# Seven block products for the up projection of MLP groups 2 to 4, and weight sums made by accumulating transfers

## Chip, core and metric

One core of a Trainium2 chip runs the whole kernel. The metric is device time in microseconds (us) from launch to end of one execution; a profiled execution is recorded beside the timed ones. TensorE is PE in the profile (PEld its weight loads), VectorE is DVE, ScalarE is ACT, GpSimd is POOL, SyncE is SP.

## What is computed

One decoder layer on 512 tokens of width 1024, all float32. The part after the token mixing is what changes most:

```python
merged = (sigmoid(ga + b_ga) * (y_a @ w_branch[0])
          + sigmoid(gb + b_gb) * (y_b @ w_branch[1])
          + sigmoid(gc + b_gc) * (y_c @ w_branch[2]))
x = layer_norm(ALPHA * x + merged @ w_o, ln1_g, ln1_b)
h = square(relu(x @ w_up))                       # w_up (1024, 4096)
x = layer_norm(ALPHA * x + h @ w_down, ln2_g, ln2_b)   # w_down (4096, 1024)
```

`ga`, `gb` and `gc` are gate columns of an input projection of x; y_a, y_b, y_c come from a convolution, a gated recurrence and an attention into 256 memory tokens.

## The kernel before

**Operands.** Each float32 operand is split into a high part (rounded, made by ACT) and a low part (the rest, made by DVE), and each product is three matmuls, high by high, high by low, low by high (`three`, L1781 to L1783). So every matmul of a projection shows under these three lines, whatever the stage. Weights come in slabs of 1 MiB (128 partitions x 2048 floats): SP loads a slab into `raw`, ACT makes `w_hi` (L960 in the MLP), DVE makes `w_lo` (L1081), and PE waits for the count `slab_lo` before it uses the slab (`slab`, L1776).

**Seven products.** Where a product of two-by-two blocks is computed with seven block products m1 to m7 instead of eight, sums of weight blocks and sums of activation blocks ("forms") are needed. Gates 2 and 3 (`seven_gate`, `seven_product`, L2044) are computed so, with sums of weight blocks made by DVE (L1358, L1366 and others) in `gate_a` and `gate_c`. There a product is 48 matmuls of 256 columns. All down projections of the MLP are computed so too: 7 products of 2 rows of 12 matmuls, 512 columns wide.

**MLP.** It runs over 4 groups of 1024 of the 4096 hidden columns. In each group PE does the up projection as eight plain tiles (`up_tile`, L2160: 24 matmuls of 512 columns each, all 512 tokens), then the seven down products (`down`, L2193). Of the first group's up projection the first four tiles are computed in token halves, beside the layer norm. ACT squares each pair of tiles (L1003 to L1015), DVE makes the forms of a quarter of the group from them (`forms`, L1608 to L1611) and their low parts, and DVE also makes four sums of 1 MiB weight blocks for the down products (`sum_of`, L1602: x12 on `small`, x4 with `raw`). A down product's result leaves PSUM by `down_add` (L1642), in the order m1, m5, m6, m3, m2, m7, m4. In the last group the order of rows is `LAST_ROWS`, and DVE takes the layer norm's statistics (L1648) as each block is complete. Weight slots are four in the MLP, three in the gates.

**POOL.** It makes the split of the memory keys and values for each of two halves (L619, L621), clears `merged` (L639), scales the residual by ALPHA once layer norm 1 has been transposed (L643, counted in `resid_ready`, for which every `down_add` waits), and at the end scales and shifts five of the eight output half blocks (L650, L653). It issues no transfer. All transfers are SP's, in program order, each behind the wait for its buffer.

Of the kernel before, what the change touches and what calls it, by code (L numbers as in the profile page):

```python
# [24 lines left out]
P = 128  # L25
T = 512
# [28 lines left out]
S_MLP, N_MLP = S_OUT + 4, 11  # L55
# [21 lines left out]
UP_SLABS = 4  # L77
# [5 lines left out]

SHARED = ((2, 0), (2, 1), (3, 0), (3, 1), (0, 0))
# [3 lines left out]
LAST_ROWS = (("m3", 0), ("m2", 0), ("m3", 1), ("m2", 1), ("m7", 0), ("m4", 0), ("m7", 1), ("m4", 1))  # L88


def made(g, name, r):

    at = 2 * PRODUCTS.index(name) + r
    if g == G_MLP - 1 and (name, r) in LAST_ROWS:
        at = 2 * len(PRODUCTS) - len(LAST_ROWS) + LAST_ROWS.index((name, r))
    return 2 * len(PRODUCTS) * g + at + 1


SUMS = ("m5", "m6", "m7", "m4")


def aside(g, name):

    return g == G_MLP - 1 and name == "m2"
# [39 lines left out]
def down_bank(g, name):  # L144
    return 2 if g == G_MLP - 1 and name == "m4" else DOWN_BANK[name]


def down_slab(g, name):
    return S_MLP + g * N_MLP + UP_SLABS + PRODUCTS.index(name)

# [34 lines left out]
def build(nc, x, mem, lower_bounds, w_in, conv_w, hg_norm_w, w_mem_k, w_mem_v, w_branch, b_gate, w_o,  # L185
          ln1_g, ln1_b, w_up, w_down, ln2_g, ln2_b, out):
    ds = bass.ds
    with ExitStack() as ctx:
# [49 lines left out]
        h_forms = two[:, 4:6, :].rearrange("p a (b t) -> p (a b) t", t=T // 2)[:, 0:7, :]  # L238
# [19 lines left out]
        form_of = dict(m7=gate_a[:, 0:1024], m6=gate_a[:, 1024:2048], m5=gate_b[:, 0:1024], m3=gate_b[:, 1024:2048])  # L258
        small = sb("small", [P, 9 * 1024])
# [18 lines left out]
        raw_a = small[:, 0:SLAB]  # L278
        raw_b = small[:, SLAB:2 * SLAB]
        raw_c = small[:, 2 * SLAB:3 * SLAB]  # L280
        late = small[:, 8192:9216].rearrange("p (c t) -> p c t", t=256)
        early = two[:, 4, :].rearrange("p (c t) -> p c t", t=256)
        h_kept = small[:, 8192:9216].rearrange("p (j t) -> p j t", j=PAIRS)
        aside_hi, aside_lo = (t[:, 0:PAIRS, :].rearrange("p k c -> p (k c)") for t in (x_hi, x_lo))
# [51 lines left out]
        a_landed, b_landed = sem("a_landed"), sem("b_landed")  # L336
        c_landed, sums_made = sem("c_landed"), sem("sums_made")
        up_done, up_read = sem("up_done"), sem("up_read")
        h_squared, form_step, forms_made = sem("h_squared"), sem("form_step"), sem("forms_made")
        forms_hi, forms_ready = sem("forms_hi"), sem("forms_ready")  # L340
        kept_hi, kept_ready = sem("kept_hi"), sem("kept_ready")
        down_done, down_read = sem("down_done"), sem("down_read")
# [15 lines left out]
        def moved_par(n, e):  # L358
            return [bank[DOWN_BANK[name] + r] for name, r, m, f in MOVED if (m, f) == (n, e)][0]
# [10 lines left out]
        def mlp_round(g):  # L370
            return g * 4 + 20

# [23 lines left out]
        wdn = w_down[0].rearrange("(k two p) c -> p two k c", two=2, p=P)  # L396

        def down_block(g, k, n):

            return wdn[:, k - 1, g * PAIRS:(g + 1) * PAIRS, (n - 1) * WID:n * WID]  # L400
# [14 lines left out]

        def direct_slab(g, d):

            return S_MLP + g * N_MLP + d if d < UP_SLABS else down_slab(g, "m2")

        @block.sync  # L420
        def _(sp):
# [116 lines left out]
            sp.wait_ge(gate_done, seven_done(2, "m6", 1))  # L538
            par_load(2, ln2_g)
            par_load(3, ln2_b)  # L540
            def direct(g, d, src, k):

                n = R_MLP + 5 * g + d
                if n < R_MLP + 2:
                    sp.wait_ge(slab_lo, S_MLP - 2 + d + 1)
                else:
                    before = 5 * g + d - 2
                    sp.wait_ge(slab_lo, direct_slab(before // 5, before % 5) + 1)
                sp.dma_start(raw[:, n % 2, :].rearrange("p (k c) -> p k c", k=k), src).then_inc(slab_landed[n % 2], 16)

            def up_load(g, j):
                direct(g, j, wup[:, :, g * D + j * 256:g * D + (j + 1) * 256], KD)

            for g in range(G_MLP):
                up_load(g, 0)
                up_load(g, 1)
                if g == 0:
                    sp.wait_ge(merged_split, KD)
                else:
                    sp.wait_ge(slab_lo, down_slab(g - 1, "m4") + 1)  # L560
                sp.dma_start(as_block(raw_a), down_block(g, 1, 1)).then_inc(a_landed, 16)
                if g:
                    sp.wait_ge(sums_made, 4 * g)
                sp.dma_start(as_block(raw_b), down_block(g, 2, 2)).then_inc(b_landed, 16)
                if g == 0:
                    sp.wait_ge(x1_ready, 2 * TB)
                else:
                    sp.wait_ge(slab_lo, down_slab(g - 1, "m7") + 1)
                sp.dma_start(as_block(raw_c), down_block(g, 1, 2)).then_inc(c_landed, 16)
                up_load(g, 2)  # L570
                up_load(g, 3)
                direct(g, 4, down_block(g, 2, 1), PAIRS)
# [17 lines left out]
        def _(pool):  # L590
# [25 lines left out]

            for half in range(2):
# [1628 lines left out]
```

## Time and profile before

| | us |
|---|---|
| median of 3 runs | 820.9 |
| lowest, highest | 820.64, 821.03 |
| the profiled execution, its own time | 820.31 |
| its span, first to last instruction | 818.5 |

The span is what the trace covers; about 1.8 us of the profiled execution's time lie around it. PE is busy 99% of the span at a granted clock of 0.997 of full speed, DVE 67%, ACT 46%, POOL 4%. Matmul durations in the trace overlap, since matmuls are pipelined and their ends are modelled: 390 ns is given for one of 512 columns, while the next starts much sooner. What a matmul costs is the distance between starts. The chain of work that ended last, followed back from the end, lies on PE almost throughout; that of waits lists, for each pair of instructions, how long an engine stood idle before one until the other had finished.

### The profile page before, as it was taken

The page shows a single profiled execution, that of the slowest core. Times are in us where ns is not written, and L with a number is a line of the kernel's source. Part 1 is how long each engine was busy: PE and PEld are TensorE (multiplying, and loading weights), DVE is VectorE, ACT ScalarE, POOL GpSimd, SP SyncE. Part 2 cuts the span into 40 slices and gives each one's busy share as a digit, 9 for nine tenths or more (in the row PEclk, how much of TensorE's full clock was granted, in tenths as well). Part 3 has the DMA queues.
Part 4 walks back from the last instruction along what each step waited for, and adds up shares of the span by engine and source line. Part 5 has one row for each costly group of instructions (what it writes and reads, how often), then busy time and mean ns, then how long its engine had stood idle before and what let it go on. Part 6 is the DMA issues. An engine that isn't in the chain of part 4 may idle for free.

```text
span 818.5 us, 10651 instructions
## 1 busy us (share of the span) xinstructions
PE 809.0 (99%) x4347; PEld 698.9 (85%) x4347; DVE 551.1 (67%) x612; ACT 375.3 (46%) x439; POOL 32.1 (4%) x40
## 2 busy tenths in 40 slices
PE   8999999999999999999999999999999999999996
PEld 8889888899888889989988899888888888888885
DVE  4647655477358628768567686986588658855887
ACT  5558324493435324443453036643554355435533
POOL 1100100000001000000000010000000000000006
PEclk9999999999999999999999999999999999999998
DMA  9641313313120730620647116028102810280002
GB/s 309 207 154 52 103 52 102 102 51 102 51 76 28 257 103 1 223 87 1 207 154 246 63 39 219 1 68 293 51 1 70 289 52 1 73 287 1 1 0 104
DMA packets 64207, 87.64 MB, mean 107 GB/s; under 512 B 1661, under 2 KB 43686, under 8 KB 64166
## 3 DMA queue, kind: packets, MB, share of 16 engines
q1 hardware_dynamic: 64166, 87.06, 31.6%
q8 instruction: 30, 0.49, 0.2%
q14 instruction: 11, 0.09, 0.0%
HBM read 84.96 MB, written 2.10 MB: 106 GB/s over the span
## 4 chain that ended last, share of the span: by engine, by line
PE 98%; DVE 1%; DMA 1%; SPq 0%; DVEq 0%; issue 0%
PE bank L1781 31%; PE bank L1782 31%; PE bank L1783 31%; DMA two<-in_mem_dram 1%; PE bank L1997 0%; PE bank L1947 0%; PE bank L1918 0%; PE bank L2117 0%; PE bank L1808 0%; PE bank L2000 0%; PE bank L1985 0%; PE bank L1949 0%; PE bank L1954 0%; PE bank L1975 0%; PE bank L1800 0%; DVE smx L1648 0%
## 5 line engine op out<-in xcount | busy, mean ns | idle before, releaser
L1781 PE MATMUL bank<-x_hi,w_hi 128*128 128x512 f32 (+1 forms) x672 | 245.7, 366 | 0.0
L1782 PE MATMUL bank<-x_lo,w_hi 128*128 128x512 f32 (+1 forms) x672 | 244.6, 364 | 0.0
L1783 PE MATMUL bank<-x_hi,w_lo 128*128 128x512 f32 (+1 forms) x672 | 244.5, 364 | 0.0
L1783 PEld LDWEIGHTS bank<-x_hi,w_lo 128*128 128x128 f32 x672 | 126.8, 189 | 20.0
L1781 PEld LDWEIGHTS bank<-x_hi,w_hi 128*128 128x128 f32 x672 | 126.8, 189 | 19.9
L1782 PEld LDWEIGHTS bank<-x_lo,w_hi 128*128 128x128 f32 x672 | 126.9, 189 | 19.5
L1781 PE MATMUL bank<-w_hi,y_hi 128*128 128x512 f32 x296 | 115.5, 390 | 0.0
L1783 PE MATMUL bank<-w_hi,y_lo 128*128 128x512 f32 x296 | 115.2, 389 | 0.0
L1782 PE MATMUL bank<-w_lo,y_hi 128*128 128x512 f32 x296 | 115.2, 389 | 0.0
L1081 DVE TENSOR_TENSOR w_lo<-raw,w_hi 128x2048 fp32r<-128x2048 f32 (+2 forms) x35 | 71.5, 2046 | 35.1 <-ACT w_hi L960 25.3
L1783 PEld LDWEIGHTS bank<-w_hi,y_lo 128*128 128x128 f32 x296 | 55.6, 188 | 11.5
L1781 PEld LDWEIGHTS bank<-w_hi,y_hi 128*128 128x128 f32 x296 | 55.6, 188 | 11.5
L1782 PEld LDWEIGHTS bank<-w_lo,y_hi 128*128 128x128 f32 x296 | 55.6, 188 | 11.4
L1081 DVE TENSOR_TENSOR w_lo<-small,w_hi 128x2048 fp32r<-128x2048 f32 (+1 forms) x28 | 59.8, 2138 | 3.4 <-ACT w_hi L686 1.4
L960 ACT ACTIVATE w_hi<-raw 128x2048 fp32r<-128x2048 f32 x17 | 32.6, 1918 | 63.0 <-PE bank L1783 41.8
L1076 DVE TENSOR_TENSOR w_lo<-raw,w_hi 128x2048 fp32r<-128x2048 f32 x22 | 50.4, 2296 | 15.6 <-ACT w_hi L665 15.3
L960 ACT ACTIVATE w_hi<-small 128x2048 fp32r<-128x2048 f32 x24 | 45.8, 1906 | 10.2 <-PE bank L1783 10.2
L1642 DVE TENSOR_TENSOR two<-two,bank 128x512 f32<-128x512 f32 x56 | 38.3, 684 | 15.9 <-PE bank L1783 10.4
L665 ACT ACTIVATE w_hi<-raw 128x2048 fp32r<-128x2048 f32 x22 | 42.2, 1919 | 11.8 <-DMA raw<-in_w_branch_dram 11.1
L1781 PE MATMUL bank<-y_hi,w_hi 128*128 128x512 f32 (+1 forms) x128 | 46.8, 366 | 0.1
L1782 PE MATMUL bank<-y_lo,w_hi 128*128 128x512 f32 (+1 forms) x128 | 46.4, 363 | 0.0
L1783 PE MATMUL bank<-y_hi,w_lo 128*128 128x512 f32 (+1 forms) x128 | 46.4, 362 | 0.0
(253 smaller groups left out, 1145.2 us busy)
## 6 DMA issues: line engine op xcount, KB each, us to landing
raw<-in_w_in_dram SPq DMA_DIRECT2D x22, 1024.0 KB, 5.1
raw<-in_w_up_dram SPq DMA_DIRECT2D x16, 1024.0 KB, 6.9
small<-in_w_down_dram SPq DMA_DIRECT2D x12, 1024.0 KB, 7.5
raw<-in_w_branch_dram SPq DMA_DIRECT2D x6, 1024.0 KB, 4.9
two<-in_x_dram SPq DMA_DIRECT2D x4, 1024.0 KB, 8.0
raw<-in_w_o_dram SPq DMA_DIRECT2D x4, 1024.0 KB, 4.9
raw<-in_w_down_dram SPq DMA_DIRECT2D x4, 1024.0 KB, 4.6
small<-in_w_mem_v_dram SPq DMA_DIRECT2D x4, 512.0 KB, 10.6
```

What stands on the lines that cost most here:

```text
L665: act.activation(w_hi[:, slot, :], raw[:, r, :], ACT.Copy).then_inc(slab_hi, 1)
L960: act.activation(w_hi[:, (s - S_MLP) % 4, :], src, ACT.Copy).then_inc(slab_hi, 1)
L1076: dve.tensor_tensor(w_lo[:, slot, :], raw[:, r, :], w_hi[:, slot, :].bitcast(F32), ALU.subtract)\
L1081: return dve.tensor_tensor(dst, src, high.bitcast(F32), ALU.subtract)
L1642: dve.tensor_tensor(z, z, bank[down_bank(g, name) + r], op).then_inc(down_read, 1)
L1781: pe.matmul(dst, a[0], b[0], start=first, stop=False, skip_group_check=goes_on)
L1782: pe.matmul(dst, a[0], b[1], start=False, stop=False, skip_group_check=goes_on)
L1783: return pe.matmul(dst, a[1], b[0], start=False, stop=last, skip_group_check=goes_on)
```

## The change

Groups 2 to 4 (numbered 1 to 3 in the code) compute the up projection as seven block products of 48 matmuls with 256 columns. ACT copies m1, m5 and m6 out of PSUM, DVE adds m3, m2 and m7 to the copies (`up_add`), ACT applies relu and square to whole blocks of 1024 columns (h11, h12, h22, h21), and DVE makes the forms of whole blocks once the last of them (from m4) is squared (`form`). For these products the forms of x are made once, in the first group (`x1_forms`, `x1_forms_low`, 8 and 4 DVE operations of 1024 columns).

The weight sums of all up and down products are no longer made by DVE. POOL issues, per job (one projection of one group; seven jobs), four copies of 1 MiB weight blocks from DRAM to an internal DRAM tensor `kept`, and four steps in which one 1 MiB block is added to another inside `kept` by two accumulating transfers in pieces of 2 KB. Each step waits for the one before. Jobs 0 and 1 start after POOL's first half, jobs 2 to 5 follow, then the scaling of the residual, then job 6. SP loads the finished sums from `kept` as ordinary slabs. The MLP now has three weight slots and three raw buffers (the third in `gate_a`). The down products run in the order m1, m2, m5, m6, m3, m7, m4.

Gate 1's products are written straight into `merged`, so the clearing and 8 DVE additions fall away.

```diff
-S_MLP, N_MLP = S_OUT + 4, 11
+S_MLP = S_OUT + 4
...
+SUM_BEGINS = dict(m5=(1, 1), m7=(1, 2), m6=(2, 2), m4=(2, 1))
+SUM_STEPS = (("m5", "m7"), ("m7", "m6"), ("m6", "m5"), ("m4", "m6"))
+JOBS = (("down", 0), ("up", 1), ("down", 1), ("up", 2), ("down", 2), ("up", 3), ("down", 3))
...
-LAST_ROWS = (("m3", 0), ("m2", 0), ("m3", 1), ("m2", 1), ("m7", 0), ("m4", 0), ("m7", 1), ("m4", 1))
+LAST_ROWS = (("m6", 0), ("m3", 0), ("m6", 1), ("m3", 1), ("m7", 0), ("m4", 0), ("m7", 1), ("m4", 1))
...
+            def make_sums(jobs, steps):
+                for n in steps:
+                    to, other = SUM_STEPS[n]
+                    for j in jobs:
+                        pool.wait_ge(kept_made[j], 16 * (len(SUMS) + 2 * n))
+                        for k in (0, 2):
+                            pool.dma_start(kept_sum(j, to)[:, k:k + 2, :], kept_sum(j, other)[:, k:k + 2, :],
+                                           accum_op=ALU.add, max_dma_last_dim=2048).then_inc(kept_made[j], 16)
...
+                if half == 0:
+                    pool.wait_ge(x_landed[1], 16)
+                    pool.wait_ge(value_landed[3], 16)
+                    begin_sums((0, 1))
+                    make_sums((0, 1), (0, 1))
+                else:
+                    make_sums((0, 1), (2, 3))
-            pool.wait_ge(branch_split, 8)
-            pool.memset(merged, 0.0).then_inc(merge_done, 1)
+            for jobs in ((2, 3), (4, 5)):
+                begin_sums(jobs)
+                make_sums(jobs, range(4))
             for b in range(TB):
                 pool.wait_ge(aux_done, LNT.done("x%d1" % b))
                 pool.tensor_scalar(resid[:, b, :], resid[:, b, :], ALPHA, 1.0, ALU.mult, ALU.mult)\
                     .then_inc(resid_ready, 1)
+            begin_sums((6,))
+            make_sums((6,), range(4))
...
+            def mlp_hi(n):
+                if n == 2:
+                    act.wait_ge(tile_done, mlp_round(0) * MAIN)
+                elif n > 2:
+                    act.wait_ge(mlp_done, slab_over(n - 3))
+                mlp_landed(act, n)
+                act.activation(w_hi[:, n % 3, :], mlp_raw(n), ACT.Copy).then_inc(slab_hi, 1)
...
+            def down(g):
+                form(g, "m5")
+                form(g, "m7")
+                mlp_lo(down_slab(g, "m5"))
+                form_to_lo(g, "m5")
+                form(g, "m6")
+                form(g, "m3")
+                mlp_lo(down_slab(g, "m6"))
+                form_to_lo(g, "m6")
+                down_add(g, "m1", 0)
+                down_add(g, "m1", 1)
+                form_to_lo(g, "m3")
+                mlp_lo(down_slab(g, "m3"))
+                down_add(g, "m5", 0)
+                down_add(g, "m5", 1)
...
+            def up_product(g, name):
+                n = up_slab(g, name)
+                slab(S_MLP + n)
+                for p in range(2):
+                    up_ready(g, name, p)
+                    for c in range(2):
+                        for k in range(PAIRS):
...
+                            mm = three(dst, w_part(n % 3, k * WID + (2 * p + c) * P, P), b,
+                                       opens and c == 0 and k == 0, k == PAIRS - 1, not opens or c == 1)
+                    mm.then_inc(mlp_done, 1)
```

On PE, where the down products of the first group end and the up projection of the second begins, the order before is this (`y_hi`, `y_lo` hold the forms of h, `x_hi`, `x_lo` the normalized x):

```order
L1782 MATMUL bank<-w_lo,y_hi 128x512
L1783 MATMUL bank<-w_hi,y_lo 128x512
L1781 MATMUL bank<-x_hi,w_hi 128x512
L1782 MATMUL bank<-x_lo,w_hi 128x512
L1783 MATMUL bank<-x_hi,w_lo 128x512
```

and after the change:

```order
L1950 MATMUL bank<-w_lo,y_hi 128x512
L1951 MATMUL bank<-w_hi,y_lo 128x512
L1949 MATMUL bank<-x_hi,w_hi 128x256
L1950 MATMUL bank<-x_lo,w_hi 128x256
L1951 MATMUL bank<-x_hi,w_lo 128x256
```

Before, 192 rows of 512 columns follow until the next down products; now 336 rows of 256 columns. Nothing else on PE is added or taken away.

On POOL, before, the second half's splits are followed by the clearing and the scaling:

```order
L619 CAST y_hi<-small 128x512
L621 TENSOR_TENSOR y_lo<-small,y_hi 128x512
L619 CAST y_hi<-small 128x512
L621 TENSOR_TENSOR y_lo<-small,y_hi 128x512
L639 MEMSET small 128x4096
L643 TENSOR_SCALAR two<-two 128x1024 x4
```

After, between the first half's splits and the scaling (two rows of splits are inside):

```order
L687 DMA kept<-in_w_down_dram 512x1x512 x4
L687 DMA kept<-in_w_up_dram 512x1x512 x4
L697 DMA kept<-kept 128x2x512 x8
L702 CAST y_hi<-small 128x512
L704 TENSOR_TENSOR y_lo<-small,y_hi 128x512
L702 CAST y_hi<-small 128x512
L704 TENSOR_TENSOR y_lo<-small,y_hi 128x512
L697 DMA kept<-kept 128x2x512 x8
L687 DMA kept<-in_w_down_dram 512x1x512 x4
L687 DMA kept<-in_w_up_dram 512x1x512 x4
L697 DMA kept<-kept 128x2x512 x16
```

The scaling has moved behind 24 copies and 48 accumulating transfers.

On DVE in the last group, before, only one slab is still to be split once the first block statistics begin (L1648 in the profile, `BN_STATS` here):

```order
L1648 BN_STATS decay<-two 128x6
L1081 TENSOR_TENSOR w_lo<-small,w_hi 128x2048
L1642 TENSOR_TENSOR two<-two,bank 128x512
L1648 BN_STATS decay<-two 128x6
L1651 BN_AGGR lbw<-decay 128x2
L1656 RECIPROCAL lbw<-lbw 128x1
L1642 TENSOR_TENSOR two<-two,bank 128x512
```

After, from the additions of m5 and m2 on (`gate_b` holds the form of m7, `small` that of m4):

```order
L1786 TENSOR_TENSOR two<-two,bank 128x512 x3
L1792 BN_STATS decay<-two 128x6
L1786 TENSOR_TENSOR two<-two,bank 128x512
L1792 BN_STATS decay<-two 128x6
L1221 TENSOR_TENSOR w_lo<-raw,w_hi 128x2048
L1786 TENSOR_TENSOR two<-two,bank 128x512 x2
L1792 BN_STATS decay<-two 128x6
L1795 BN_AGGR lbw<-decay 128x2
L1221 TENSOR_TENSOR y_lo<-gate_b,y_hi 128x1024
L1800 RECIPROCAL lbw<-lbw 128x1
L1221 TENSOR_TENSOR y_lo<-small,y_hi 128x1024
L1786 TENSOR_TENSOR two<-two,bank 128x512
```

The next row there is the split of the last slab (m4's). Two slabs and two forms' low parts now stand among the statistics.

## Rows read from the trace of the kernel before

**Rows 1.** the page: busy us by engine (1), the chain that ended last (4)

```profile
PE 809.0 (99%) x4347; PEld 698.9 (85%) x4347; DVE 551.1 (67%) x612; ACT 375.3 (46%) x439; POOL 32.1 (4%) x40
...
PE 98%; DVE 1%; DMA 1%; SPq 0%; DVEq 0%; issue 0%
```

**Rows 2.** timeline of PE: start us, us, line, operation, shapes, count

```profile
566.36 0.39 PE L1781 MATMUL bank<-x_hi,w_hi 128*128 128x512 f32 x1
...
609.88 0.39 PE L1781 MATMUL bank<-w_hi,y_hi 128*128 128x512 f32 x1
...
647.96 0.39 PE L1781 MATMUL bank<-x_hi,w_hi 128*128 128x512 f32 x1
...
810.93 0.39 PE L1783 MATMUL bank<-w_hi,y_lo 128*128 128x512 f32 x1
```

**Rows 3.** timeline of PE, 256 columns wide, in the seven-product gate stage

```profile
317.89 0.28 PE L1781 MATMUL bank<-x_forms_b,w_hi 128*128 128x256 f32 x1
...
323.65 0.28 PE L1781 MATMUL bank<-x_forms_b,w_hi 128*128 128x256 f32 x1
```

**Rows 4.** instructions grouped by line and shape: count, busy us, mean ns, idle before

```profile
L1081 DVE TENSOR_TENSOR w_lo<-raw,w_hi 128x2048 fp32r<-128x2048 f32 x29 | 66.3, 2290 | 34.4 <-ACT w_hi L960 25.3 <-ACT w_hi L823 9.0
...
L1642 DVE TENSOR_TENSOR two<-two,bank 128x512 f32<-128x512 f32 x56 | 38.3, 684 | 15.9 <-PE bank L1783 10.4 <-issue 3.5
...
L1602 DVE TENSOR_TENSOR small<-small 128x2048 f32<-128x2048 f32 x12 | 27.2, 2283 | 0.0
```

**Rows 5.** timelines of ACT and DVE in the last group: operations 1024 columns wide

```profile
782.80 1.06 ACT L1032 ACTIVATE y_hi<-small 128x1024 fp32r<-128x1024 f32 x1 [3.13 <-PE bank L1783]
...
785.62 1.22 DVE L1081 TENSOR_TENSOR y_lo<-small,y_hi 128x1024 fp32r<-128x1024 f32 x1
```

**Rows 6.** timeline of DVE at the end of the last group

```profile
793.21 0.69 DVE L1648 BATCH_NORM_STATS2 decay<-two 128x6 f32<-128x512 f32 x1
793.94 2.29 DVE L1081 TENSOR_TENSOR w_lo<-small,w_hi 128x2048 fp32r<-128x2048 f32 x1
...
808.70 0.69 DVE L1640 TENSOR_TENSOR two<-two,bank 128x512 f32<-128x512 f32 x1
...
811.42 0.69 DVE L1642 TENSOR_TENSOR two<-two,bank 128x512 f32<-128x512 f32 x1
```

**Rows 7.** stretches: busy us by engine, PEclk, DMA share, GB/s

```profile
37.00:250.00 213.00, 213.00 (x1230) 184.94 (x1229) 123.90 (x179) 105.50 (x144) 4.74 (x5) 1.00 0.27 87
...
300.00:363.00 63.00, 63.00 (x437) 59.00 (x436) 44.97 (x39) 25.83 (x27) 0.00 (x0) 1.00 0.35 118
```

**Rows 8.** DMA, 270 to 310 us: GB/s in 40 slices; us to landing

```profile
GB/s 0 0 0 25 205 371 391 309 362 340 354 399 401 408 406 219 20 0 0 8 264 397 379 0 0 0 0 0 0 0 0 0 54 265 325 363 58 0 0 0
...
gate_b<-in_w_in_dram SPq DMA_DIRECT2D x1, 1024.0 KB, 8.3
...
gate_c<-in_w_in_dram SPq DMA_DIRECT2D x2, 512.0 KB, 4.8
```

**Rows 9.** timelines of SP, ACT and DVE around the first seven-product gate

```profile
301.45 0.92 SPq L499 DMA_DIRECT2D gate_c<-in_w_in_dram  x2
...
284.31 1.92 ACT L665 ACTIVATE w_hi<-raw 128x2048 fp32r<-128x2048 f32 x1 [11.10 <-DMA raw<-in_w_branch_dram]
...
308.30 1.22 DVE L1358 TENSOR_TENSOR gate_a<-gate_a,gate_c 128x1024 f32<-128x1024 f32 x1
...
320.56 2.29 DVE L1081 TENSOR_TENSOR w_lo<-gate_a,w_hi 128x2048 fp32r<-128x2048 f32 x1 [2.04 <-ACT w_hi L843]
```

**Rows 10.** timelines of POOL (36.10 ends its first half) and PE

```profile
36.10 1.29 POOL L621 TENSOR_TENSOR y_lo<-small,y_hi 128x512 fp32r<-128x512 f32 x1
...
86.74 1.14 POOL L619 CAST y_hi<-small 128x512 fp32r<-128x512 f32 x1 [25.07 <-PE bank L1783]
...
162.72 0.28 PE L1782 MATMUL bank<-y_lo,y_hi 128*128 128x256 f32 x1
...
459.28 1.05 POOL L643 TENSOR_SCALAR two<-two 128x1024 f32<-128x1024 f32 x1 [202.17 <-PE bank L2117]
```

More of the change, by code:

```diff
@@ new lines, in _ @@
+            for j in range(4):
+                at = (j // 2) * (DFF // 2) + (j % 2) * 256
+                mlp_load(j, wup[:, :, at:at + 256], KD)
+            for g in range(G_MLP):
+                if g:
+                    for name in PRODUCTS:
+                        product_load("up", g, name)
+                for name in ROWS:
+                    if g == G_MLP - 1 and name == "m6":
+                        sp.wait_ge(mlp_done, slab_done(up_slab(g, "m3"), 1))
+                        par_load(2, ln2_g)
+                        par_load(3, ln2_b)
+                    product_load("down", g, name)
@@ L1064, in _, with mark, marked, activated @@
-            for g in range(G_MLP):
-                mlp(g)
+            steps = [0]
+            def mark(ins):
+                ins.then_inc(act_step, 1)
+                steps[0] += 1
+            def marked():
+                act.wait_ge(act_step, steps[0])
+            def activated(z):
+                mark(act.activation(z, z, ACT.Relu))
+                marked()
+                return act.activation(z, z, ACT.Square)
+            def form_to_hi(g, name):
+                act.activation(form_hi[:, FORM_OF[name], :], h_of[name], ACT.Copy).then_inc(forms_hi, 1)
@@ L1068, in _ @@
+            last_blocks()
         @block.vector
@@ L1755, in last_rows @@
                 norm_two(0, 1)
-            for g in range(G_MLP):
-                mlp(g, g == G_MLP - 1)
+            plain_up()
+            down(0)
+            for g in range(1, G_MLP):
+                seven_up(g)
+                down(g)
         @block.tensor
@@ new lines, in _, with up_ready @@
+            for u in range(4, 8):
+                pe.wait_ge(up_read, u - MAIN + 1)
+                if u % 2 == 0:
+                    slab(S_MLP + u // 2)
+                feature_part(bank[u % MAIN], slice(0, T), (u // 2) % 3, u % 2).then_inc(mlp_done, 1)
+            def up_ready(g, name, p):
+                if name == "m1":
+                    pe.wait_ge(down_read, made(g - 1, "m3", p))
+                elif name == "m2":
+                    pe.wait_ge(down_read, made(g - 1, "m2", p))
+                elif name == "m5" and g == 1:
+                    pe.wait_ge(up_read, 8)
+                elif name == "m5":
+                    pe.wait_ge(up_added, up_added_of(g - 1, "m3", p))
+                elif name == "m4":
+                    pe.wait_ge(up_added, up_added_of(g, "m7", p))
+                else:
+                    pe.wait_ge(up_read, up_read_of(g, LAST_READ[name], p))
@@ L2219, in _ @@
-            for g in range(G_MLP):
-                for u in range(MAIN if g == 0 else 0, 8):
-                    up_tile(g, u)
-                down(g)
+                elif name == "m5" and g == 0:
+                    pe.wait_ge(up_read, 5 + r)
+                elif name == "m5":
+                    pe.wait_ge(up_read, up_read_of(g, "m4", r))
+                elif g and name == "m2":
+                    pe.wait_ge(up_added, up_added_of(g, "m2", r))
+                elif g:
+                    pe.wait_ge(down_read, made(g - 1, "m4", r))
@@ new lines, in row @@
+            def row(g, name, r):
+                n = down_slab(g, name)
+                slab(S_MLP + n)
+                pe.wait_ge(forms_ready, form_ready(g, name))
+                down_ready(g, name, r)
+                opens = name in DOWN_OPENS or down_bank(g, name) != ROW_BANK[name]
+                for j in range(PAIRS):
+                    mm = three(bank[down_bank(g, name) + r],
+                               both(form_hi, form_lo, ALL, FORM_OF[name], slice(j * 256 + r * P, j * 256 + (r + 1) * P)),
+                               w_part(n % 3, j * WID, WID), opens and j == 0, j == PAIRS - 1, not opens)
+                mm.then_inc(mlp_done, 1)
@@ L2226 @@
+            for g in range(G_MLP):
+                if g:
+                    for name in PRODUCTS:
+                        up_product(g, name)
+                last = g == G_MLP - 1
+                for name in ROWS[0:3 if last else 7]:
+                    for r in range(2):
+                        row(g, name, r)
+                if last:
+                    for name, r in LAST_ROWS:
+                        row(g, name, r)
 _INS = ["x", "mem", "lower_bounds", "w_in", "conv_w", "hg_norm_w", "w_mem_k", "w_mem_v", "w_branch", "b_gate",
```

628 lines of the change are left out of this document (330 added, 298 removed).

## The prediction, made before the changed kernel ran

> **What bounds the kernel now.** The page comes first, then PE's timeline at the borders of the stages, then the rows of the engines that feed it. PE is busy 99% of the span, 98% of the chain that ended last lies on PE, and the granted clock is near 1 throughout [rows 1, 7]. So only two things count: PE's own work, and new moments in which PE waits. DVE (67%) and ACT (46%) are not the bound; a gain there is worth nothing unless they were late. The sum is made against the profiled execution's 820.31 us; the median, 820.9, lies 0.6 above it, and that is added at the end.
>
> **PE's work.** One up projection is 192 matmuls of 512 columns, from 566.36 to 609.88 [rows 2]: 43.52 us, 0.2267 each. A down projection after it is 168 such matmuls: 38.08 us to 647.96 [rows 2], and stays. The new up projection is seven products of 48 matmuls of 256 columns. The gates have just that: 5.76 us from one product to the next [rows 3], 0.1200 each, so 336 x 0.1200 = 40.32 us. Half the columns cost more than half the time. Per group 43.52 - 40.32 = 3.2 us, for three groups **-9.6**. The orders give 336 rows for 192, so the count is sure.
>
> The spacing in the rows is 5% above half for half the columns (0.1200 against 0.1134). The Trainium skill, TensorE: Matmul & The Clock Gate, section "Back-to-back issue gap", would have less for both widths (columns at 2.4 GHz and 2.5 ns more); by it the saving would be 4.7 us a group, 14 in all. The rows include what it leaves out, and decide: 9.6.
>
> **DVE's and ACT's work.** DVE loses the sums (twelve of 2.28 us and four like them [rows 4]) and gains one weight split of 2.29 [rows 4] for each summed block it now takes as a slab like any other: 14 slabs a group. This is hidden as long as no step stands before PE's need, so I worked DVE's order through from T = start of a group's down products. Prices: split 2.2 from issue to issue, a form or its low part 1.1 to 1.2 (the 1024-wide rows [rows 5]), ACT square or rounding 1.06 [rows 5], an addition 0.68 [rows 4] (0.8 in a row of them), statistics 0.73 [rows 6], PE's end to another engine's start 0.26.
>
> *Groups 2 and 3.* The last up product's block is squared at T+1.95. Then forms m5 and m7 and the split of m5 end at 6.7, its form's low part at 7.8, where PE comes to m5 at 10.9; m6 at 13.6 for 16.3; m3's split at 18.5 for 21.8; m7's and m4's parts run out almost level: m4 row 0 is ready at 32.4, PE wants it at 32.6, row 1 at 35.4 for 35.4. **+0.2** for both. *Group 1* has the old up stage, whose last tile must go through relu, square and two forms first: the same chain 1.4 us later, which the level end does not absorb: **+1.5** (bounds 0 and 3).
>
> *Last group.* Here the statistics stand between, and the order gives two forms' low parts and two splits after the first of them, where before there was one split at 793.94 and none later [rows 6]. From T: additions and statistics of m2 end at 23.0, split of m7 25.2, m6 row 0, m3 row 0 and its statistics 27.5, low part of m7's form 28.95. PE wants m7 row 0 at 27.2: a wait of 1.8. Low part of m4's form, one addition, split of m4: 33.3, where PE wants m4 row 0 at 31.7: a wait of 1.6. PE's last row ends at 41.5 instead of 38.1. DVE then still has four additions, three statistics and one scaled addition (8 x 0.73) and four small operations, to 40.1; then m7 row 1, and 2.72 later (808.70 to 811.42 [rows 6]) m4 row 1, at 42.8. Before it was T+38.3. So **+4.5**; bounds 0 (the relative lateness of two engines is the least sure thing here, each step 5% off moves it 1.5) and 6.
>
> **Transfers.** 28 MiB are copied from DRAM to `kept` and 28 MiB accumulated there; then the loads are as before plus the up slabs' sums, in a kernel whose DMA share is about a third [rows 7]. Full traffic runs at about 400 GB/s [rows 8], so 1 MiB copied holds all 16 engines 2.6 us. No row shows an accumulating transfer. Below it costs what a copy does (2.6); above there is no bound from a row; it reads two operands, and I take twice, 5.2. Jobs 0 to 5 are 24 copies (63 us) and 24 accumulations (126): 189 us of all engines. Loads take 0.27 to 0.35 [rows 7], so they need 189/0.7 = 270 us plus some 35 for 24 steps that each wait for the one before: from 37.4, the end of POOL's first half [rows 10], to about 340. So they lie beside all loads of the branches and gates.
>
> The place where a slower load hurts is the first seven-product gate. SP asks for `gate_c` at 301.45 [rows 9], it lands 4.8 to 5.4 us later [rows 8], DVE adds it at 308.30, and the last split of that chain ends at 322.85 [rows 9], for a product that starts at 323.65 [rows 3]: 0.8 us to spare, plus about 2.1 of DVE operations that the direct write into `merged` takes away: 2.9. With equal shares to two streams its 2.6 us of data become 5.7, 3.1 later: **+0.2**; if the sums get two shares of three, 6.2 later and +3.3. ACT already waited 11.10 us for a branch slab [rows 9] without PE waiting: earlier loads have slack.
>
> The Trainium skill, DMA: Bandwidth & Descriptors, section "Issuing engines are not separate DMA queues", says that transfers from any engine end on the same 16 engines and interleave: no separate path for POOL's traffic. Its page Collectives: The Full Stack, section on the bandwidth ceiling, has a reducing transfer at half the rate of a plain one since it reads two sources (62.28 against 32.35 GB/s). No run here shows either. By one rate for both, the sums would end near 250, before the gate.
>
> **POOL's queue.** Waits for each step block what stands behind. The second half's splits stand behind steps 0 and 1 of the first two jobs; the last of them ran at 86.74, and PE reads the half's first from 162.72 on [rows 10]. Jobs 0 and 1 have finished step 1, 8 copies and 4 accumulations, (21 + 21)/0.7 + 3 = 63 us after 37.4, at about 100: hidden. The residual's scaling (459.28, four of 1.05 [rows 10]) now stands behind jobs 0 to 5; the first `down_add` wants it near 540. At 340 that is hidden, 0. The clearing, the 8 DVE additions in the gates and the larger ACT squares are under work that was never late: 0.
>
> **Sum.** 820.31 - 9.6 + 0.2 + 1.5 + 4.5 + 0.2 = 817.1; with 0.6, **817.7**.
>
> **Rivals.**
> (a) *No wait in the last group.* PE's starting point of that stage could slip by less, or ACT and DVE be quicker than worked out: then 4.5 falls away: 813.2. For it: before, DVE had idle time there. Against: the order puts both splits late.
> (b) *Moderate contention.* Loads get a third of the engines at the first seven-product gate: +3.3 for 0.2, so 820.8: no change.
> (c) *Heavy contention.* The pieces of 2 KB are short, and an accumulation may hold an engine longer than its bytes say. Loads at a third of their rate anywhere from 60 to 340 us turn a 1 MiB slab of 2.6 us into 8, against 5.76 us of PE work per product [rows 3]. The branch load that was 11.1 us late and harmless would come later still. Several waits, 3 to 12 us, I take 8: 825.7, slower. 2.9 us of slack at 301 decides; above it each microsecond of delay is one of PE.
> (d) *POOL late*, the other side by much. The budget from 37.4 to 540 is 502 us; less 24 copies (63/0.7 = 90) it is 17 us for each of 24 accumulations. My estimate is 5.2/0.7 + 1.5 = 9. If one takes 19, the scaling comes at 590, all `down_add` and so PSUM wait, and the sums for later groups are late too: 850 or more. It begins at 17.
> (e) *PSUM chain of the up products* (copy by ACT, additions by DVE) longer than a product: an addition and a copy take 0.68 [rows 4] and at most 1.06 [rows 5] against a product's 5.76 us; excluded.
>
> **Chances.** Forecast 0.38, (a) 0.12, (b) 0.15, (c) 0.20, (d) 0.15. The low end is (a) less 0.7; the high end takes in (c) with 3 more: 812.5 to 829, leaving out most of (d) and the worst of (c). About 0.2% (1.6 us) is what a measurement tells from no change, so the forecast itself is near that bound: 817.7 is 0.4% faster. Faster: (a), nine tenths of the forecast: 0.47. Same: (b) and a little of the forecast: 0.18. Slower: (c) and (d): 0.35.
>
> **What the profile after would show.** Right: up stages of 40.3 us with 0.120 between starts; down stages 38.1 except the first (1.5 longer) and the last; in the last group waits of PE's m7 and m4 rows on DVE (`y_lo`, `w_lo`) of about 1.8 and 1.6, and the last addition 4.5 later after T than before; PE without a gap near 318 to 324; DMA share near 1 until about 340; POOL's scaling there. Wrong: PE gaps ended by a DMA or by ACT's `w_hi` between 60 and 340 (c), a scaling after 540 with PE waiting on `bank` (d), a down stage of 38.1 at the end (a), or starts in the up stage that are not 0.120 apart, which would undo the only gain in the sum.

## The result, and the profile after

| | before | after |
|---|---|---|
| median | 820.83 us (4 runs) | 839.54 us (4 runs) |
| lowest, highest | 820.64, 821.03 | 834.1, 841.54 |
| the profiled execution, its own time | 820.31 | 841.54 |

Ratio 1.0217, 95% interval 1.017 to 1.0265: the changed kernel is 2.2% slower, with the whole interval on the slower side, where 817.7 was forecast. Its runs also lie 7.4 us apart, those of before 0.4.

The page of the changed kernel, busy time by engine and the shares of the chain that ended last [rows 1]:

```profile
PE 804.4 (96%) x4779; PEld 714.0 (85%) x4779; DVE 551.4 (66%) x587; ACT 403.2 (48%) x457; POOL 117.9 (14%) x123
...
issue 54%; PE 30%; POOL 10%; DVE 4%; DMA 1%; ACT 0%; SPq 0%; DVEq 0%; POOLq 0%
```

PE had 98% of that chain and has 30% now. "issue" is time in which an engine waited for nothing that the profile shows, and with POOL beside it this is POOL's issuing of transfers. What PE itself waited for (engine, line, what it waited for: us in total, times, longest):

```profile
PE bank L1949 <- DVE two L1786: 22.7, 1, 22.7
PE bank L1949 <- DVE w_lo L1221: 1.8, 1, 1.8
PE bank L1983 <- POOL ident L664: 1.5, 1, 1.5
PE bank L1949 <- issue: 1.1, 1, 1.1
```

One wait of 22.7 us is longer than the whole loss. L1786 is `down_add`. PE's timeline (start, duration) at the two borders of that stage (compare [rows 2]) and at that place in it:

```profile
529.29 0.39 PE L1949 MATMUL bank<-w_hi,y_hi 128*128 128x512 f32 x1
...
545.38 0.39 PE L1951 MATMUL bank<-w_hi,y_lo 128*128 128x512 f32 x1
568.50 0.77 PE L1949 MATMUL bank<-w_hi,y_hi 128*128 128x512 f32 x1 [22.73 <-DVE two L1786]
569.06 0.63 PE L1950 MATMUL bank<-w_lo,y_hi 128*128 128x512 f32 x1
...
592.98 0.28 PE L1949 MATMUL bank<-x_hi,w_hi 128*128 128x256 f32 x1
```

POOL's timeline just ahead of it, its last accumulating transfers of jobs 4 and 5 and the scaling of the residual (L734; 459.28 in [rows 10]):

```profile
538.00 1.15 POOL L697 DMA_DIRECT2D kept<-kept  x1 [4.81 <-issue]
547.49 1.15 POOL L697 DMA_DIRECT2D kept<-kept  x1 [8.34 <-issue]
555.32 1.15 POOL L697 DMA_DIRECT2D kept<-kept  x1 [6.68 <-issue]
563.11 1.15 POOL L697 DMA_DIRECT2D kept<-kept  x1 [6.65 <-issue]
564.34 4.42 POOL L734 TENSOR_SCALAR two<-two 128x1024 f32<-128x1024 f32 x4
```

DVE's first `down_add` behind it:

```profile
567.66 0.69 DVE L1786 TENSOR_TENSOR two<-two,bank 128x512 f32<-128x512 f32 x1 [23.53 <-POOL two L734]
```

The scaling could have run from 460 to 494. It ran at 564.34, behind the sums; `down_add` had been ready for it since 544.1, the results stayed in PSUM, and PE stood for want of a free bank. The stretches (us from and to, length, busy us and count of PE, PEld, DVE, ACT, POOL, then PEclk, DMA share, GB/s) show what else this cost:

```profile
545.50:568.50 23.00, 0.27 (x3) 0.03 (x1) 0.69 (x1) 1.91 (x1) 7.38 (x7) 0.60 0.61 105
568.50:573.00 4.50, 4.50 (x11) 3.53 (x12) 4.21 (x4) 0.00 (x0) 1.05 (x2) 0.50 0.38 47
```

After 23 us without work the granted clock is 0.50, the lower of the two levels (1.2 GHz), and for 12 matmuls the distance between starts is 0.43 us instead of 0.227: 2.6 us more.

**The account.** From PE's timelines, stage by stage, after less before:

| stretch | before | after | difference |
|---|---|---|---|
| start to first down product | 528.28 | 529.29 | +1.0 |
| down products, group 1 | 38.08 | 63.69 | +25.6 |
| three up projections | 3 x 43.52 | 3 x 40.31 | -9.6 |
| down products, groups 2 and 3 | 2 x 38.08 | 38.10 + 38.11 | +0.05 |
| last group, T to its last addition | 38.34 | 42.51 | +4.2 |
| sum | | | +21.2 |

and 841.54 - 820.31 = 21.2. All but the second line lie within 1 us of the terms of the prediction.

### The profile page after: what moved, and what is told of

Read it like the earlier page. It is cut to its first block, busy times and chain, and to the rows that moved or that the text cites. A ratio compares the mean times of both kernels' runs of the same rounds, so it can differ in the third digit from the quotient of the medians.

```text
span 839.7 us, 11669 instructions
## 1 busy us (share of the span) xinstructions
PE 804.4 (96%) x4779; PEld 714.0 (85%) x4779; DVE 551.4 (66%) x587; ACT 403.2 (48%) x457; POOL 117.9 (14%) x123
## 3 DMA queue, kind: packets, MB, share of 16 engines
q0 software_dynamic: 22848, 58.73, 34.4%
## 4 chain that ended last, share of the span: by engine, by line
issue 54%; PE 30%; POOL 10%; DVE 4%; DMA 1%; ACT 0%; SPq 0%; DVEq 0%; POOLq 0%
PE bank L1949 10%; PE bank L1950 10%; PE bank L1951 10%; POOL kept L697 7%; POOL kept L687 2%; DVE two L1786 1%; DVE w_lo L1221 1%; POOL y_lo L704 1%; DMA two<-in_mem_dram 1%; DVE y_lo L1221 0%; PE bank L1976 0%; POOL two L734 0%; DVE decay L1792 0%; DVE smx L1792 0%; POOL y_hi L702 0%
## 5 line engine op out<-in xcount | busy, mean ns | idle before, releaser
L1949 PE MATMUL bank<-x_hi,w_hi 128*128 128x512 f32 (+1 forms) x624 | 211.8, 339 | 0.0
L1950 PE MATMUL bank<-x_lo,w_hi 128*128 128x512 f32 (+1 forms) x624 | 210.6, 338 | 0.0
L1951 PE MATMUL bank<-x_hi,w_lo 128*128 128x512 f32 (+1 forms) x624 | 210.6, 338 | 0.0
L1949 PE MATMUL bank<-w_hi,y_hi 128*128 128x512 f32 x304 | 120.1, 395 | 25.7 <-DVE two L1786 22.7
L1221 DVE TENSOR_TENSOR w_lo<-raw,w_hi 128x2048 fp32r<-128x2048 f32 (+2 forms) x52 | 111.2, 2140 | 37.8 <-ACT w_hi L1050 28.7
L697 POOL DMA_DIRECT2D kept<-kept x56 | 64.6, 1153 | 361.3 <-issue 331.4
L1050 ACT ACTIVATE w_hi<-raw 128x2048 fp32r<-128x2048 f32 x36 | 68.7, 1912 | 80.3 <-PE bank L1951 75.7
L1221 DVE TENSOR_TENSOR w_lo<-gate_a,w_hi 128x2048 fp32r<-128x2048 f32 x25 | 57.2, 2289 | 25.5 <-ACT w_hi L1050 17.8
L1950 PE MATMUL bank<-x_forms_b,w_hi 128*128 128x256 f32 x256 | 72.4, 283 | 0.0
L1786 DVE TENSOR_TENSOR two<-two,bank 128x512 f32<-128x512 f32 x56 | 38.3, 684 | 29.2 <-POOL two L734 24.0
L1949 PE MATMUL bank<-x_form_hi,w_hi 128*128 128x256 f32 x192 | 54.3, 283 | 0.0
L1951 PE MATMUL bank<-x_form_hi,w_lo 128*128 128x256 f32 x192 | 54.3, 283 | 0.0
L759 ACT ACTIVATE w_hi<-raw 128x2048 fp32r<-128x2048 f32 x22 | 42.3, 1921 | 21.4 <-DMA raw<-in_w_branch_dram 13.1
```

Of the source, the lines that this page charges most:

```text
L697: pool.dma_start(kept_sum(j, to)[:, k:k + 2, :], kept_sum(j, other)[:, k:k + 2, :], accum_op=ALU.add, max_dma_last_dim=2048).then_inc(kept ...
L759: act.activation(w_hi[:, slot, :], raw[:, r, :], ACT.Copy).then_inc(slab_hi, 1)
L1050: act.activation(w_hi[:, n % 3, :], mlp_raw(n), ACT.Copy).then_inc(slab_hi, 1)
L1221: return dve.tensor_tensor(dst, src, high.bitcast(F32), ALU.subtract)
L1786: dve.tensor_tensor(z, z, bank[down_bank(g, name) + r], op).then_inc(down_read, 1)
L1949: pe.matmul(dst, a[0], b[0], start=first, stop=False, skip_group_check=goes_on)
```

## The experiments

**1. The scaling moved (mid), and the accumulations left out (no_adds).** The first undoes nothing of the change but the scaling's place:

```diff
-            for jobs in ((2, 3), (4, 5)):
-                begin_sums(jobs)
-                make_sums(jobs, range(4))
+            begin_sums((2, 3))
+            make_sums((2, 3), range(4))
+            begin_sums((4, 5))
+            make_sums((4, 5), range(2))
             for b in range(TB):
                 pool.wait_ge(aux_done, LNT.done("x%d1" % b))
                 pool.tensor_scalar(resid[:, b, :], ...)
+            make_sums((4, 5), range(2, 4))
```

> The residual's scaling stands between steps 1 and 2 of the last two jobs ahead of it instead of behind all of them; nothing else is changed. Theory 1 (POOL's queue: the scaling came at 564.34, 22.7 us too late, and PE then ran 12 matmuls at 0.43 us instead of 0.23): the scaling runs near 510, PE has no wait of 22.7 us, the stage of the first down products takes 38 to 39.6 us instead of 63.7; the time falls by 25.6 us less the 0 to 1.5 us of a chain that lay under the stall: 816 to 817.5. Rival (contention: loads and not the place in the queue made down_add late, or the loss would move to another place): PE waits turn up elsewhere, 825 or more.

Measured: 816.62 us (5 runs, 815.99 to 816.84; before 820.66 on the same chip), ratio 0.9949, interval 0.9936 to 0.9963. PE's longest waits are these (the view of waits, then the place of the last one in PE's timeline, in the first group):

```profile
PE bank L1951 <- DVE w_lo L1223: 2.1, 2, 1.8
PE bank L1985 <- POOL ident L664: 1.5, 1, 1.5
PE bank L1951 <- issue: 1.1, 1, 1.1
PE bank L1951 <- DVE two L1788: 0.3, 1, 0.3
```

```profile
561.04 0.39 PE L1953 MATMUL bank<-w_hi,y_lo 128*128 128x512 f32 x1
561.78 0.47 PE L1951 MATMUL bank<-w_hi,y_hi 128*128 128x512 f32 x1 [0.35 <-DVE two L1788]
```

and POOL's timeline has the scaling between two steps:

```profile
494.25 1.15 POOL L697 DMA_DIRECT2D kept<-kept  x1 [9.24 <-issue]
495.47 8.82 POOL L735 TENSOR_SCALAR two<-two 128x1024 f32<-128x1024 f32 x4
504.35 1.17 POOL L697 DMA_DIRECT2D kept<-kept  x1
```

The first down stage takes 38.78 us instead of 63.69. So the position of one operation in POOL's queue is worth 22.9 us between the medians (24.9 in this stage of the profiled executions), and the rest of the change is 4.0 us faster than the kernel before.

> All accumulating transfers are left out (the copies stay, so products use unsummed weight blocks; the output is not the reference's), the scaling stays behind the jobs. Theory 1: POOL reaches the scaling after 24 copies of 6.1 us, before 300, so there is no stall and the time is 816 to 817.5, as with the scaling moved. If the transfers' traffic on the shared engines costs PE anything besides (the stages from 269 to 330 were 0.34 us longer than before), this run is shorter than the moved one by that, under 1 us. Rival: the weight loads' delay from the accumulations is worth several us: 812 or less.

Measured: 816.11 us, one run. With 28 MiB of accumulations gone from the 16 engines the kernel is 0.5 us shorter than mid, which is inside the 0.9 us over which mid's runs spread. Contention, as far as it reaches PE, costs nothing that can be told here. Loads do take longer beside the accumulations: the median from issue to landing of an input-projection slab is 5.2 us in no_adds and 7.5 in the changed kernel, and PE doesn't wait for them in either.

**2. What paces POOL's transfers (pieces4k, quarter).** In the changed kernel POOL's rows ahead show one transfer, a pause of 5 to 9 us, the next. The program waits only between steps: there is no wait between the copies, and they too stand 6.8 us apart, while one takes about 6 us to land; nor is there one between the two transfers of a step, and these stand 7.9 us apart, no closer than two of different steps (7.4). So the waits of the program do not pace the queue. The edits (in quarter the counts that a step waits for are raised to four transfers per step):

```diff
-                                           accum_op=ALU.add, max_dma_last_dim=2048).then_inc(kept_made[j], 16)
+                                           accum_op=ALU.add, max_dma_last_dim=4096).then_inc(kept_made[j], 16)
```

```diff
-                        for k in (0, 2):
-                            pool.dma_start(kept_sum(j, to)[:, k:k + 2, :], kept_sum(j, other)[:, k:k + 2, :],
+                        for k in range(4):
+                            pool.dma_start(kept_sum(j, to)[:, k:k + 1, :], kept_sum(j, other)[:, k:k + 1, :],
```

> The accumulating transfers go in pieces of 4 KB instead of 2 KB, all else as in the changed kernel. What paces POOL's transfers, three theories: (A) room for pieces in the queue: half the pieces, so two transfers are in flight, issues stand 4 us apart instead of 7.7 and the scaling comes before 480; time 816. (B) one transfer at a time whatever its pieces: spacing stays equal to the landing time, 7 to 7.7; time near 840. (C) the DMA engines' time per piece: 7.0 us of all engines per MiB falls towards 4, landing from 7.6 to 5 or less, the scaling comes 60 to 100 us earlier; time 816.

> Each step's 1 MiB goes in four accumulating transfers of 256 KB instead of two of 512 KB, pieces of 2 KB as before. (A) Room for pieces decides: issues 3.9 us apart, each lands after more than its spacing (two in flight), 1 MiB still takes 15.4, time near 840. (B) One transfer at a time: each takes a fixed part of about 2 us plus half of the rest, 4.8, so 1 MiB takes 19 us instead of 15.4; the scaling comes 24 x 4 = 90 us later and the time is 920 or more.

Measured: 816.93 and 820.67 us (one run each). POOL's timeline of pieces4k at the end of jobs 4 and 5, then that of quarter in jobs 0 and 1 (xN: so many issues in a row without a pause):

```profile
354.56 1.65 POOL L697 DMA_DIRECT2D kept<-kept  x2 [6.83 <-issue]
363.93 1.69 POOL L697 DMA_DIRECT2D kept<-kept  x2 [7.72 <-issue]
372.15 1.65 POOL L697 DMA_DIRECT2D kept<-kept  x2 [6.53 <-issue]
380.48 0.84 POOL L697 DMA_DIRECT2D kept<-kept  x1 [6.67 <-issue]
```

```profile
149.36 2.50 POOL L697 DMA_DIRECT2D kept<-kept  x3 [6.09 <-issue]
154.75 0.83 POOL L697 DMA_DIRECT2D kept<-kept  x1 [2.89 <-issue]
162.00 2.53 POOL L697 DMA_DIRECT2D kept<-kept  x3 [6.42 <-issue]
```

With half the pieces per transfer, two and three go out in a row and several are in flight at once; POOL is done with jobs 0 to 5 at 381 in pieces4k, 183 us earlier than in the changed kernel. So theory B falls with both kernels, and the number of pieces in a transfer decides whether another goes out beside it, as A has it. What each view says of landing and of the engines' time, changed kernel, pieces4k, quarter, from the page's DMA part (kind, KB each, median us to landing; kind, packets, MB, share of the 16 engines):

```profile
kept<-kept POOLq DMA_DIRECT2D x56, 512.0 KB, 7.6
q0 software_dynamic: 22848, 58.73, 34.4%
```

```profile
kept<-kept POOLq DMA_DIRECT2D x56, 512.0 KB, 8.9
q0 software_dynamic: 15680, 58.73, 31.7%
```

```profile
kept<-kept POOLq DMA_DIRECT2D x112, 256.0 KB, 7.0
q0 software_dynamic: 23744, 58.73, 33.6%
```

Copies alone (no_adds: 10.3% of 814.3 us for 28 MiB) hold the engines 3.0 us per MiB. The rest of q0 is the accumulations, if copies cost the same beside them: (0.344 x 839.7 - 84) / 28 = 7.3 us per MiB with pieces of 2 KB, 6.2 with 4 KB. For 24 accumulations that is 26 us less, where POOL was 183 us earlier, and the landing time rose from 7.6 to 8.9 us where C wanted 5 or less. So C explains a small part at most.

The packets give the pieces. no_adds has 7616 on q0 for 28 copies, 272 each. The accumulating transfers have the rest: (22848 - 7616) / 56 = 272 each in the changed kernel, 144 in pieces4k, and (23744 - 7616) / 112 = 144 in quarter (512 KB in pieces of 2 KB are 256, half of that in number are 128, and each transfer has 16 more). Copies and accumulations of 272 packets both go out singly, at different sizes (1 MiB and 512 KB); those of 144 do not. But at 144 each, pieces4k sends two in a row and quarter three, then one. A count of pieces alone does not give that, and how room comes free again stays open.

Quarter was forecast wrongly under both theories (840 or 920). More is in flight, but an accumulated MiB still takes 13.8 us (from the first issue of each batch to POOL's next operation, for 15.1 before; A had 15.4), and the copies end sooner, since the first accumulation goes out right behind the last copy. The scaling comes at 501.85, 62 us earlier, and that is early enough: no stall of PSUM. But quarter shows another wait. Its DVE timeline at the first seven-product gate [rows 9]:

```profile
313.95 2.36 DVE L1498 TENSOR_TENSOR gate_a<-gate_a,gate_c 128x1024 f32<-128x1024 f32 x2 [5.80 <-DMA gate_c<-in_w_in_dram]
316.23 0.68 DVE L1553 TENSOR_TENSOR small<-two,bank 128x512 f32<-128x512 f32 x1
318.63 2.29 DVE L1221 TENSOR_TENSOR w_lo<-gate_a,w_hi 128x2048 fp32r<-128x2048 f32 x1 [1.72 <-ACT w_hi L937]
```

`gate_c` landed up to 11.5 us after its issue, and PE waited 2.44 us for this split, while accumulations were under way. Behind the wait the granted clock was 0.50 again, and 13 matmuls of 256 columns stood 0.21 us apart instead of 0.12, 1.2 us more. The 3.6 us together are rival (b) of the prediction, at its place and near its price (3.3), in one run and with denser traffic than the change has.

**3. The last group (tail_order, tail_pool, best).** tail_order is mid with another order in `last_rows`:

```diff
-                complete("m2", 0)
-                complete("m2", 1)
+                down_add(g, "m2", 0)
+                down_add(g, "m2", 1)
                 mlp_lo(down_slab(g, "m7"))
-                down_add(g, "m6", 0)
-                complete("m3", 0)
-                moments(0, 2)
                 form_to_lo(g, "m7")
-                scales(0)
+                down_add(g, "m6", 0)
+                down_add(g, "m3", 0)
                 form_to_lo(g, "m4")
                 down_add(g, "m6", 1)
                 mlp_lo(down_slab(g, "m4"))
+                half_stats(g, "m2", 0)
+                half_stats(g, "m2", 1)
+                half_stats(g, "m3", 0)
+                moments(0, 2)
+                scales(0)
```

> Base is the kernel with the scaling moved (mid, 816.62). In the last group DVE takes the statistics of m2 and m3 row 0 only after the split of m4's slab, so that the splits and the forms' low parts that PE needs come 2.3 us and more earlier; no work is taken away. Theory T (DVE's amount of work sets the end): PE's waits of 1.1 and 1.8 us before m7 and m4 shrink below 0.5, but from the first down addition on DVE is busy without a break, so the last addition of m4 row 1 stays at T+42.5: the time stays within 0.5 us of 816.6. Rival O (the order, that is PE's two waits, sets the end): 3.2 us less, 813.4.

Measured: 817.9 us, ratio 0.997 (0.996 to 0.9981). So rival O (813.4) falls; theory T wanted 816.6 within 0.5, and the time is 1.3 us above it. PE's two waits are gone, and its last group takes 38.35 us instead of 41.70. The end came no earlier: DVE's last addition is at 807.93, T+43.3, where mid has T+42.5. DVE's timeline shows where the added 0.8 went, two waits on ACT for the deferred block scales (1.89 us, where mid has 0.36):

```profile
797.34 0.16 DVE L1802 RECIPROCAL lbw<-lbw 128x1 f32<-128x1 f32 x1 [0.42 <-ACT lbw L1168]
...
800.64 0.16 DVE L1802 RECIPROCAL lbw<-lbw 128x1 f32<-128x1 f32 x1 [1.47 <-ACT lbw L1168]
...
807.93 0.68 DVE L1788 TENSOR_TENSOR two<-two,bank 128x512 f32<-128x512 f32 x1
```

The two waits are 1.5 us more than in mid. Of that 0.8 came back, for DVE's last split takes 2.29 us here and 3.13 in mid, where POOL's first output operation ran beside it. Mid's timelines of DVE and of POOL there:

```profile
794.74 3.13 DVE L1223 TENSOR_TENSOR w_lo<-raw,w_hi 128x2048 fp32r<-128x2048 f32 x1
```

```profile
794.43 1.29 POOL L746 TENSOR_TENSOR two<-two,small 128x512 f32<-128x512 f32 x1 [125.88 <-ACT two L1180]
795.80 3.22 POOL L749 TENSOR_TENSOR two<-two,small 128x512 f32<-128x512 f32 x1
```

So 3.35 us of PE's time saved bought nothing: PE's end does not set the end of this stretch, the chain on DVE does, its work and, in tail_order, its waits on ACT. Stretches of mid and of the kernel before, from T+13.4 to the last addition, say the same (columns as above):

```profile
777.97:807.76 29.79, 25.51 (x110) 20.05 (x108) 28.38 (x38) 12.35 (x21) 13.02 (x9) 1.00 0.16 62
```

```profile
786.49:812.11 25.62, 24.83 (x110) 20.24 (x108) 19.98 (x30) 9.84 (x19) 12.01 (x10) 1.00 0.11 42
```

DVE is busy 95% of it, against 78% before, with 8.4 us more busy time (0.84 of them the slowed split). This supports theory T. That the stretch gets shorter when DVE has less work was to be tested by the next run.

> As tail_order, and POOL makes the low parts of the forms m7, m3 and m4 of the last group (three of about 2.6 us on an idle engine) in place of DVE (three of 1.13 us). Theory T: DVE's end comes 3.4 us earlier until PE's own end (T+38.3) sets it: last addition near T+39, time 813.2. Rival O: no gain over tail_order. Third: POOL and DVE hinder each other (POOL's 1.29 us splits took up to 3.2 us beside DVE), low parts come too late for m3 at T+21.8: PE waits there, 815 or more.

Its edit: for the last group `form_to_lo` of m7, m3 and m4 is issued on POOL and counted by a semaphore of its own.

Measured: 820.89 us, ratio 1.0006 (0.9997 to 1.0015). The third case: the two engines hinder each other. POOL's and DVE's timelines:

```profile
778.69 3.29 POOL L749 TENSOR_TENSOR y_lo<-two,y_hi 128x1024 fp32r<-128x1024 f32 x1 [4.65 <-ACT y_hi L1096]
781.95 3.36 POOL L749 TENSOR_TENSOR y_lo<-small,y_hi 128x1024 fp32r<-128x1024 f32 x1
```

```profile
779.64 3.43 DVE L1233 TENSOR_TENSOR y_lo<-two,y_hi 128x1024 fp32r<-128x1024 f32 x1
782.99 1.50 DVE L1798 TENSOR_TENSOR two<-two,bank 128x512 f32<-128x512 f32 x2
784.40 3.06 DVE L1233 TENSOR_TENSOR w_lo<-gate_a,w_hi 128x2048 fp32r<-128x2048 f32 x1
```

DVE's 1024-wide low part takes 3.43 us beside POOL's, where it takes 1.22 alone [rows 5], and a split 3.06 for 2.29; DVE's additions that read PSUM (1.50 for two) are not slowed. The ends show how: POOL's first low part ends at 781.98 and DVE's, begun beside it, 1.09 us later; POOL's next ends at 785.31 and DVE's split 2.15 later. In mid the split ends 2.15 us after POOL's 1.29. Each time the later one took about its whole time after the earlier had ended, so the two took turns and did not share. Another of DVE's low parts was slowed in the same way (3.42 us at 771.70), so DVE lost 2.2 + 2.2 + 0.8 us and was spared 3 x 1.13. The test of theory T by less work for DVE thus did not take place. DVE's additions came late, PE waited 2.13 and 1.43 us for them (and not for m3's low part, as the third case had it), and the last addition stands at 811.51, T+46.3. The Trainium skill, SBUF — State Buffer, section "Who interferes with whom", says that a two-input DVE operation with both inputs in SBUF contends with GpSimd's reads; these rows agree with it.

> As tail_pool, with accumulating transfers in pieces of 4 KB instead of 2 KB. In the kernel where only the pieces were changed POOL was done with jobs 0 to 5 near 381 instead of 564, so here the place of the scaling no longer matters; the first weight loads meet denser traffic. Expected the same as tail_pool within 0.8 us: 813.2 to 814; the wait of 0.46 us at 386 and up to 1 us between 262 and 300 may show again.

Measured: 821.15 us, ratio 1.0005 (0.9996 to 1.0014), the same as tail_pool, with the same waits of PE (2.13 and 1.39), and not the 813.2 to 814 expected. The fastest kernel of the study that makes its sums is mid, with pieces4k 0.3 us behind it (one run).

## Why the prediction was wrong

**The step that failed** is the size of one term: the wall time of POOL's sums. The prediction had 2.6/0.7 = 3.7 us for a copy and 9 us for an accumulated MiB, so that jobs 0 to 5 would end near 340. Measured on POOL's timeline, from issue to issue: 6.8 us for a copy and 15.1 for an accumulated MiB (two transfers of 7.56 us), 24 x 6.8 + 24 x 15.1 = 526 us from 38.0 to 564.3. Two things are in it. The engines' time was 7.3 us per accumulated MiB, not 5.2, inside "2.6 to no upper bound", and 3.0 per copy, not 2.6: by the prediction's own sum that makes 24 x 3.0 + 24 x 0.6 = some 85 us of the 224 between 340 and 564. The larger part was left out: the sum divided engine time by the free share, as if transfers followed each other without a gap, while with these sizes POOL sends one at a time and each pays nearly its whole time to landing. The sign "DMA share near 1 until about 340" failed with it: the share was 0.75 from 38 to 340. In pieces4k it was 0.90 up to 381, and an accumulated MiB takes 8.5 us ((69.6 + 68.4 + 66.8)/24, from the first issue of each of the three batches to POOL's next operation), near the 9 that were forecast. The profile of before had a hint, in [rows 8]: two loads of 512 KB land 4.8 us after their issue, one of 1 MiB 8.3 (part of it behind others), against 2.6 us of data.

**The rival that happened** is (d), POOL late. Its place, its mechanism, its sign (a scaling after 540 with PE waiting on `bank`) and its budget were right: the residual was wanted near 544, the budget of 502 us is what 24 x 6.8 + 24 x 14.1 fill, and 526 were used. Its threshold of 17 us for each accumulation was too high, because a copy was put at 3.75: with copies at 6.8 it begins at 14.1, and 15.1 crossed it. "850 or more" was worked out for a scaling at 590. It came at 564, and the loss is the distance by which POOL was late, 22.7 us, and 2.6 for the clock. The sums for later groups, late too by that rival, cost PE no wait. It had a chance of 0.15 and was kept out of the range. It deserved more: between a term with no upper bound and a threshold at twice its estimate, only an unseen rate stood.

**Point by point.**
- PE's work: -9.6 forecast, 3 x (43.52 - 40.31) = -9.6 measured. The estimate of 14 us from the figures of the Trainium skill, TensorE: Matmul & The Clock Gate, section "Back-to-back issue gap", was not reached; the start-to-start distance of the gate rows gives the measured saving.
- Groups 2 and 3 of the down products: +0.2 forecast, +0.05 measured.
- Group 1's chain: +1.5 forecast, +0.7 measured (38.78 in mid; it lay under the stall in the changed kernel).
- The last group: +4.5 forecast, +4.2 measured, with PE's waits of 1.1 and 1.8 us for 1.8 and 1.6. But the working called them the cause, and tail_order showed that they are not. The chain on DVE sets the end, busy for 28.4 of 29.8 us, with 0.84 us in it that POOL's output operations cost. The hand schedule contained this ("DVE then still has ...") without saying it.
- First gate's load: +0.2 forecast. From PE's start at 318.74 to that at 330.42 it is 0.16 us longer than before (317.89 to 329.41), and 0.17 more were lost from 269 to 302; which load made the latter is not shown. At the first place the size agrees by luck. DVE waited for `gate_c` there:

```profile
310.42 2.36 DVE L1498 TENSOR_TENSOR gate_a<-gate_a,gate_c 128x1024 f32<-128x1024 f32 x2 [1.92 <-DMA gate_c<-in_w_in_dram]
```

The last split of the chain ended at 324.52, when PE had reached its product, so no slack was left. The sum had counted on 2.1 us of DVE operations taken away, but from the addition to that end are 14.10 us, and 14.55 before: the chain runs through ACT's roundings and got only 0.45 shorter. And two equal streams make 5.2 us of its 2.6, not the 5.7 of the sum. Of the first line of the account, 0.7 us stand before 21 us, ahead of POOL's first transfer.
- Heavy contention (c): refuted. No gap of PE ended by a DMA or by ACT's `w_hi` between 60 and 340 in the changed kernel.
- POOL's second-half splits: they ran from 145.92 on, where the last ran at 86.74 before [rows 10], and the keys' parts were done at 149.24, 14 us before PE reads them: hidden, as forecast, but 45 us later than forecast.
- Without the stall the forecast of 817.7 would have been 1.1 us off (mid, 816.6), most of it group 1's chain.

**The spread.** The changed kernel's runs differ by 7.4 us and mid's by 0.9. Where PE waits for the end of a queue of 72 transfers, their summed landing times are in the total; that this makes the spread fits the two numbers and was not tested by itself.

## What to carry to other kernels

An operation that another engine waits for must not stand behind a batch of transfers on its queue, however much slack the batch seems to have: put it between two of them, at the time when its input is ready. When transfers are costed, ask how many are in flight: landing time one by one, or engine time when many, and here the two differ by a factor of two. And where PE waits beside a DVE that is busy 95%, another order, or a neighbour that takes turns with it, gives nothing back; what is left is less work for DVE, which no run here tried without hindering it.

## What the runs showed of the hardware

- POOL's issue of a transfer pauses where the program has no wait, and how many go out in a row depends on the pieces of a transfer, though not on them alone: accumulations of 512 KB in pieces of 2 KB (272 packets) went out singly, 7.56 us apart, and copies of 1 MiB (272 too) singly, 6.8 apart; with 4 KB (144 packets) accumulations of 512 KB went in pairs, and those of 256 KB with 2 KB (144) in threes and ones. How large the room is was not measured.
- An accumulating transfer DRAM to DRAM held the 16 engines 7.3 us per MiB (2 KB pieces), 6.8 (2 KB, 256 KB each) or 6.2 (4 KB), a copy 3.0, as worked out above.
- Two-input operations of DVE and POOL on SBUF at the same time took turns: 3.43 us for 1.22 on DVE beside 3.3 on POOL for a low part of 1024 columns, DVE's end 1.09 us after POOL's; even a 2048-wide DVE split beside one 512-wide POOL operation took 3.13 for 2.29, ending 2.15 us after it.
- After 23 us of idle PE the granted clock was 0.50 (1.2 GHz) and 12 matmuls of 512 columns stood 0.43 us apart. After a wait of 2.44 us in quarter it was 0.50 too, for 13 matmuls of 256 columns at 0.21 us. Behind the waits of 1.13 and 1.81 us in mid's last group it stayed at 1.00 over the stretch.
